# Two more adaLN blocks in the gated mixer, none in the last stages, and a pool residual without ScalarE's bias step

## The chip, the cores and the metric

The kernel runs on one core of one Trainium2 chip. The metric is the device time of one execution in microseconds (us). The median of three runs of the kernel before is 1438.69 us (1438.45 to 1440.27). All matrices are float32; the program is one straight line of instructions for each of the five engines (TensorE, VectorE, ScalarE, GpSimd, SyncE), tied together by semaphores that the author sets by hand.

## The reference

One inference step of a trunk of four layers, for 128 context tokens and 128 latent tokens with the same weights. D is 1024.

```
mod = silu(cond) @ w_ada[i] + b_ada[i]          # 1024 x 6144 per layer
sh1, sc1, g1, sh2, sc2, g2 = split(mod, 6)
h = rmsnorm(x) * norm_g * (1 + sc1) + sh1
x = x + g1 * mixer_i(h)        # 0: Hyena, 1: gated linear attention, 2: FNet, 3: pooling
h = rmsnorm(x) * norm_g * (1 + sc2) + sh2
x = x + g2 * hier_moe(h)       # 16 SwiGLU experts, hidden 512, two per token
pool mixer: y = ((window_mean(h) - h) @ pool_w + pool_b) * pool_scale
```

Each weight is read once from HBM; the profile counts 549 MB read.

## The kernel before

**Weights as pieces.** `piece_stream` (L118) writes down one order in which all weights come: pieces of 1 MB (128 partitions x 2048 floats) that SyncE loads into a ring of 14 slots. A slot is loaded again when TensorE has used what lay in it, and SyncE waits for the slots strictly in that order. From the second pair of experts on a layer loads expert pieces two at a time, as one transfer of 2 MB. Four further slabs of each layer (the second matrices of its first pair of experts) go to a place outside the ring; in layers 0 to 2 SyncE waits for a point in the mixer before it loads them.

**adaLN blocks.** w_ada is cut into 12 blocks of 2048 columns, three for each layer, and each block into 8 pieces. Block 3i gives sh1 and sc1 of layer i, block 3i+1 gives g1 and sh2, block 3i+2 gives sc2 and g2. `ada(n, lo, hi)` (L619) issues the matmuls of pieces lo to hi of block n on TensorE: four matmuls a piece (eight instructions in the profile), which write four strips of 32 partitions of one PSUM bank (line L626). When a block is complete, VectorE copies the bank to `rows` (`ada_rows`, L1370), TensorE turns it by four transposes (`ada_turned`, L630, line L634), and VectorE adds the bias and forms the scale (`ada_mod`, L1376). A new block may begin when the modulation of the block before it is formed, since it uses the same bank.

**Where they stand.** The blocks are put by hand between other work of TensorE. Block 5 and 6 lie in the projections of the gated mixer (`pe_gla`, L480): block 6 between the k and the v projections, its turn behind v, ahead of the gates of the backward direction. Block 7 lies at the mixer's end. Block 8 lies beside the norm behind the mixer and beside the routing of layer 1's experts (`residual` with beside=8, `moe(1, 8)`), with its turn behind the first gather. Layer 2 (FNet) has block 9 in the mixer and block 10 beside norm and routing. Layer 3 (pooling) has block 11 inside its mixer. Its routing has no block beside it.

**A layer's norm.** ScalarE squares x into hT, one of 8 column blocks at a time (`square`, L1087, line L1093). TensorE sums the squares over partitions with a matrix of ones (`norm`, `sum_squares`, line L640). ScalarE takes a logarithm and an exponential of the sum (`inverse_root`, L1099, lines L1101 and L1102). VectorE multiplies (L1394), then ScalarE shifts and scales the context tokens (L1115) and VectorE the latent ones (L1398). For the odd norms, those behind a mixer, GpSimd adds the squares of blocks 1 to 6 into block 0, so that TensorE sums two blocks only.

**A residual behind a mixer.** For each of the 8 column blocks m, ScalarE reads the mixer's output from PSUM, adds a bias and writes `yb` (`residual`, L1118, line L1124), VectorE adds the gated value to xT (L1401, line L1405), and ScalarE squares the new block. In the pool mixer VectorE's factor is the gate times pool_scale, and pool_b is ScalarE's bias.

**The experts.** `moe(i)` computes the routing: logits (L840), transposes of h (L845), a chain of small operations on VectorE (L1509 to L1547), and ranks (L865 to L869). The first gather (L685) selects token rows into 64 slots an expert. Then come eight pairs of experts in order (`moe_round`, L753). A pair is the first matrix (L720, 32 instructions), the scatter of the pair before (L703), the third matrix (L720), a gather for a later pair (L685), transposes (L727, L732), and the second matrix (L744, 32 instructions). At the end VectorE adds the sums from PSUM to xT (`sums_added`, line L1460).

Of the kernel before, what the change touches and what calls it, by code (L numbers as in the profile page):

```python
# [18 lines left out]
L = 128  # L19
# [18 lines left out]
COUPLES = PAIRS // 2  # L38
HALF = D // 8 + 1


# [76 lines left out]
def piece_stream():  # L118

    def ada(n, lo=0, hi=KD):  # L120
        return [("ada", n, k) for k in range(lo, hi)]

    def pieces(name, count):
        return [(name, c) for c in range(count)]

    before = [ada(0) + pieces("w_in", 12) + ada(1) + ada(2) + ada(3) + pieces("w_out", 4) + ada(4),
              ada(5, 0, 5) + pieces("wq", 2) + ada(5, 5) + pieces("wk", 2) + ada(6) + pieces("wv", 4)
              + pieces("wg", 4) + ada(7) + pieces("wo", 4) + ada(8),
              ada(9) + pieces("fn", 4) + ada(10),
              ada(11, 0, 5) + pieces("pool", 1) + ada(11, 5)]  # L130
    out, at = [], 0
    for i in range(LAYERS):
        experts = [("moe", i, p, kind, q) for p in range(PAIRS) for kind in range(3) for q in range(SLABS)
                   if p or kind < 2]
        for what in before[i] + [("first", i)] + experts + [("further", i)]:
            if what[0] in ("first", "further"):
                out.append((what, None, None))
                at += at % 2
                continue
            out.append((what, at % RING, at // RING))  # L140
            at += 1
    return out
# [11 lines left out]
def build(nc, a):  # L154
# [21 lines left out]
    with ctx:  # L176
# [35 lines left out]
        def vcol(name, lo, n=1):  # L212
            return vec[:, VEC[name] + lo:VEC[name] + lo + n]
# [266 lines left out]
        def pe_gla(pe, arrived, ada, ada_turned, norm, h_ready, project, residual):  # L480
# [25 lines left out]
            ada(6, 0, 8)  # L506
            for c in range(4):
                w8 = arrived(("wv", c), KD)
                for g in range(G):
# [6 lines left out]
                    if c % 2:  # L516
                        last.then_inc(s("gla_proj"), 1)
            ada_turned(6)
            gates(pe, 1)
            pe.wait_ge(s("v_ready"), 4)  # L520

            def g_tiles(first, end):

                pe.wait_ge(s("mod_ready"), 7)
                for m in range(first, end):
# [58 lines left out]
            pe.wait_ge(s("g_raw"), 8)  # L584
            ada(7, 0, 3)

            pe.wait_ge(s("upd_read"), 6)
            for h in range(HEADS):
# [4 lines left out]
                if h % 2:  # L593
                    last.then_inc(s("osum_mm"), 1)
            ada(7, 3, 8)
            residual(1, "wo", oT, lambda k: pe.wait_ge(s("o_ready"), k + 1), turned=7, beside=8)

# [11 lines left out]
        def _(pe):  # L609
# [35 lines left out]
            def norm(n, beside=None):  # L645

                if n % 2:
                    pe.wait_ge(s("squares_added"), (KD - 2) * (n // 2 + 1))
                for k in (0, KD - 1) if n % 2 else range(KD):
                    sum_squares(n, k)  # L650
# [343 lines left out]


            pe_gla(pe, arrived, ada, ada_turned, norm, h_ready, project, residual)
            moe(1, 8)


            ada(9, 0, 2)  # L1000
            norm(4)
            ada(9, 2, 5)
            pe.wait_ge(s("cm_loaded"), 16 * 2)
            cg = cm[:, 0:4 * HALF].rearrange("p (k n) -> p k n", k=2)
            cl, *sl = [cm[:, 4 * HALF + n * P:4 * HALF + n * P + P] for n in range(3)]
            for g in range(G):
                for r in range(4):
# [8 lines left out]
                    last.then_inc(s("mix_mm"), 1)  # L1016
            ada(9, 5, 8)
            pe.wait_ge(s("mix_rows"), 8)
            for m in range(KD):
# [5 lines left out]
                if m % 2:  # L1025
                    last.then_inc(s("mix_mm"), 1)
            ada_turned(9)
            pe.wait_ge(s("mix_rows"), 8 + 4)
            residual(2, "fn", rhs=fnm, beside=10)
            moe(2, 10)  # L1030


            ada(11, 0, 2)
            norm(6)
            ada(11, 2, 5)
            pw = arrived(("pool", 0), KD)
            pe.wait_ge(s("cm_loaded"), 16 * 3)
            for g in range(G):
                for r in range(4):
# [6 lines left out]
                    if r % 2:  # L1046
                        last.then_inc(s("mix_mm"), 1)
            ada(11, 5, 8)
            pe.wait_ge(s("mix_rows"), 12 + 4)
            for m in range(KD):  # L1050
# [3 lines left out]
                last.then_inc(s("res_mm"), 1)  # L1054
                if m == 1:
                    ada_turned(11)
            norm(7)
# [11 lines left out]
        def _(act):  # L1069
# [48 lines left out]
            def residual(i, bias, src):  # L1118
                for m in range(KD):
                    act.wait_ge(s("res_mm"), KD * i + m + 1 if i < 3 else KD * i + (m | 1) + 1)  # L1120
                    if m >= 4:
# [218 lines left out]
            for b in range(4):  # L1340
                act.wait_ge(s("mix_mm"), 12 + b + 1)
                act_fn(plr[:, b // 2, 2 * (b % 2):2 * (b % 2) + 2], bank[b][:].rearrange("p (r n) -> p r n", r=2),
                       ACT.Copy).then_inc(s("mix_rows"), 1)
            residual(3, "pool_b", half)
            moe(3)
# [10 lines left out]
        def _(dve):  # L1356
# [392 lines left out]
            v.memset(sc[:], 0.0).then_inc(s("sc_clear"), 1)  # L1749
            ada_rows(6)  # L1750
            ada_mod(6)
            scores(0)
# [15 lines left out]
            for m in range(KD):  # L1768
                dve.wait_ge(s("ors_ready"), m // 4 + 1)
                o = oT[:, m].rearrange("p g t -> p (g t)")  # L1770
                tt(o, o, ors[:, m // 2], ALU.mult).then_inc(s("o_ready"), 1)
            ada_rows(7)
            residual(1, g1(1))
            ada_mod(7)
            moe(1, 8)
            norm(4)
            ada_rows(9)
            residual(2, g1(2))
            ada_mod(9)
            moe(2, 10)  # L1780
            norm(6)
            ada_rows(11)
            ada_mod(11)

            gs = rtv(200, KD, G)
            chain(tt(gs, mod[:, 3, 16:24], vcol("pool_scale", 0, KD).unsqueeze(2).broadcast_to([P, KD, G]), ALU.mult))
            residual(3, lambda m, g: gs[:, m, g:g + 1])
            moe(3)
# [10 lines left out]
        def _(pool):  # L1799
# [17 lines left out]
            add_squares(5)  # L1817
            add_squares(7)

# [84 lines left out]
```

## Time and profile before

| | |
|---|---|
| median of 3 runs | 1438.69 us |
| the profiled execution: time, span | 1437.99 us, 1436.2 us |
| TensorE matmul busy | 1357.9 us (95%) |
| VectorE, ScalarE, GpSimd busy | 361.1, 286.8, 36.4 us |
| DMA | 552.28 MB, 385 GB/s in the mean |
| chain that ended last | PE 80%, DMA 15%, DVE 2%, ACT 1% |

The span runs from the first to the last instruction of the profile; the time of the same execution is 1.8 us longer. Names of engines in the rows are PE (TensorE's matmuls), PEld (its weight loads), DVE (VectorE), ACT (ScalarE), POOL (GpSimd) and SP (SyncE). L626 is line 626 of the kernel. A row of a timeline may merge several instructions of one kind, and its length is then that of all of them together. A matmul's length holds the time in the pipeline, so that matmuls overlap; what one costs is best read from the start of the next. The PEclk column is the granted clock of TensorE, 1.00 being 2.4 GHz and 0.50 being 1.2 GHz.

### The profile page before, as it was taken

The page shows a single profiled execution, that of the slowest core. Times are in us where ns is not written, and L with a number is a line of the kernel's source. Part 1 is how long each engine was busy: PE and PEld are TensorE (multiplying, and loading weights), DVE is VectorE, ACT ScalarE, POOL GpSimd, SP SyncE. Part 2 cuts the span into 40 slices and gives each one's busy share as a digit, 9 for nine tenths or more (in the row PEclk, how much of TensorE's full clock was granted, in tenths as well). Part 3 has the DMA queues.
Part 4 walks back from the last instruction along what each step waited for, and adds up shares of the span by engine and source line. Part 5 has one row for each costly group of instructions (what it writes and reads, how often), then busy time and mean ns, then how long its engine had stood idle before and what let it go on. Part 6 is the DMA issues. An engine that isn't in the chain of part 4 may idle for free.

```text
span 1436.2 us, 17316 instructions
## 1 busy us (share of the span) xinstructions
PE 1357.9 (95%) x7234; PEld 734.6 (51%) x7234; DVE 361.1 (25%) x883; ACT 286.8 (20%) x523; POOL 36.4 (3%) x36
## 2 busy tenths in 40 slices
PE   7999999999989999999999989999998887999986
PEld 3786584444325788774444336744443353444433
DVE  3444514112113313323111113331111144111113
ACT  3211024111102221232111004421110054111101
POOL 0001310000000000010000000100000000000000
PEclk9999999999999999999999999999999997999998
DMA  9956999999999983499999999999999999999994
GB/s 377 420 194 226 404 398 384 395 424 429 427 427 421 421 371 103 186 410 385 396 427 427 428 426 420 421 428 421 426 428 428 426 419 401 383 427 428 427 428 167
DMA packets 54213, 552.28 MB, mean 385 GB/s; under 512 B 5937, under 2 KB 7921, under 8 KB 8817
## 3 DMA queue, kind: packets, MB, share of 16 engines
q1 hardware_dynamic: 52496, 549.09, 91.8%
q10 hardware_dynamic: 1634, 2.02, 0.4%
q8 instruction: 60, 0.98, 0.3%
q14 instruction: 23, 0.19, 0.0%
HBM read 548.99 MB, written 2.10 MB: 384 GB/s over the span
## 4 chain that ended last, share of the span: by engine, by line
PE 80%; DMA 15%; DVE 2%; ACT 1%; issue 0%; POOL 0%; SPq 0%; POOLq 0%; DVEq 0%
PE bank L720 25%; PE bank L666 14%; DMA ring<-in_moe_w 12%; PE bank L744 12%; PE bank L626 5%; PE bank L685 4%; PE bank L703 3%; DMA ring<-in_pool_w 2%; PE bank L497 2%; PE bank L514 2%; PE bank L640 1%; PE bank L840 1%; PE bank L952 1%; PE bank L572 1%; PE bank L727 1%; PE bank L890 1%
## 5 line engine op out<-in xcount | busy, mean ns | idle before, releaser
L720 PE MATMUL bank<-ring,arena 128*64 128x512 f32 x1024 | 229.4, 595 | 33.0 <-DMA ring<-in_moe_w 31.4
L720 PE MATMUL bank<-ring,hT 128*64 128x512 f32 x1024 | 225.3, 594 | 0.0
L744 PE MATMUL bank<-ring,arena 128*64 128x512 f32 x896 | 198.8, 596 | 0.0
L720 PEld LDWEIGHTS bank<-ring,arena 128*64 128x64 f32 x1024 | 73.1, 137 | 181.6 <-issue 151.4
L720 PEld LDWEIGHTS bank<-ring,hT 128*64 128x64 f32 x1024 | 72.1, 137 | 139.3 <-issue 137.0
L1430 DVE TENSOR_TENSOR rows<-rows,bank 128x512 f32<-128x512 f32 x32 | 22.0, 688 | 469.4 <-PE bank L720 469.4
L744 PEld LDWEIGHTS bank<-ring,arena 128*64 128x64 f32 x896 | 61.2, 137 | 117.6 <-issue 112.0
L666 PE MATMUL bank<-hT,ring 128*128 128x256 f32 x512 | 112.4, 380 | 0.0
L666 PEld LDWEIGHTS bank<-hT,ring 128*128 128x128 f32 x512 | 96.5, 190 | 15.2 <-issue 2.5
L1152 ACT ACTIVATE yv_big<-bank,arena 128x512 fp32r<-128x512 f32 x64 | 44.0, 688 | 288.6 <-PE bank L744 288.6
L1449 DVE SCALAR_TENSOR_TENSOR yv_rest<-bank,arena,yv_big 128x512 fp32r<-128x512 f32 x64 | 48.1, 751 | 200.1 <-ACT yv_big L1152 200.1
L626 PE MATMUL bank<-ring,condT 128*32 128x512 f32 x768 | 91.1, 602 | 6.5 <-DMA ring<-in_w_ada 4.8
L666 PE MATMUL bank<-arena,ring 128*128 128x256 f32 x384 | 83.8, 380 | 1.2 <-DVE arena L1642 0.9
L666 PEld LDWEIGHTS bank<-arena,ring 128*128 128x128 f32 x384 | 72.6, 190 | 12.2 <-DVE arena L1642 1.2
L685 PE MATMUL bank<-sel,htok_big 128*128 128x256 f32 x256 | 69.4, 305 | 1.7 <-DVE sel L1417 1.7
L703 PE MATMUL bank<-selT,yv_big 128*128 128x256 f32 x256 | 66.6, 297 | 1.7 <-DVE yv_rest L1449 1.7
L685 PE MATMUL bank<-sel,htok_rest 128*128 128x256 f32 x256 | 64.6, 286 | 0.0
L703 PEld LDWEIGHTS bank<-selT,yv_big 128*128 128x128 f32 x256 | 48.0, 187 | 28.5 <-issue 26.0
L703 PE MATMUL bank<-selT,yv_rest 128*128 128x256 f32 x256 | 62.1, 279 | 0.0
L685 PEld LDWEIGHTS bank<-sel,htok_big 128*128 128x128 f32 x256 | 49.4, 193 | 23.9 <-issue 20.7
L1145 ACT ACTIVATE rows<-bank 128x512 f32<-128x512 f32 x32 | 19.1, 597 | 211.4 <-PE bank L720 211.4
L1135 ACT ACTIVATE arena<-bank 128x512 f32<-128x512 f32 x32 | 19.1, 598 | 157.9 <-PE bank L685 157.9
(215 smaller groups left out, 1225.7 us busy)
## 6 DMA issues: line engine op xcount, KB each, us to landing
ring<-in_moe_w SPq DMA_DIRECT2D x166, 2048.0 KB, 19.4
ring<-in_w_ada SPq DMA_DIRECT2D x96, 1024.0 KB, 22.5
ring<-in_moe_w SPq DMA_DIRECT2D x36, 1024.0 KB, 20.3
arena<-in_moe_w SPq DMA_DIRECT2D x16, 1024.0 KB, 19.6
ring<-in_hy_w_in SPq DMA_DIRECT2D x12, 1024.0 KB, 28.0
ring<-in_hy_w_out SPq DMA_DIRECT2D x4, 1024.0 KB, 12.0
ring<-in_gla_w_v SPq DMA_DIRECT2D x4, 1024.0 KB, 22.7
ring<-in_gla_w_g SPq DMA_DIRECT2D x4, 1024.0 KB, 16.5
```

The source lines that it names most:

```text
L497: last = mm(half(4 * w + h), w8[:, k, (h % 2) * P:(h % 2) * P + P], hT[:, k].rearrange("p g t -> p (g t)"), start=k == 0, stop=k == KD - 1)
L514: last = mm(bank[b][:, 256 * (c % 2):256 * (c % 2) + 256], hT[:, k, g], w8[:, k, :], start=k == 0, stop=k == KD - 1)
L626: last = mm(ada_bank(n)[32 * j:32 * j + 32, :], condT[:, G * k:G * k + 32], w[:, j, :], start=k == 0, stop=k == KD - 1)
L666: last = mm(dst, w[:, k, (m % 2) * P:(m % 2) * P + P], (hT[:, k] if rhs is None else rhs[:, k]).rearrange("p g t -> p (g t)"), start=k == ...
L685: last = mm(bank[b][:, (k % 2) * NT:(k % 2) * NT + NT], htok[n % 2][:, n // 2, k * P:k * P + P], sel[:, n // 2].rearrange("p e j n -> p (e ...
L703: last = mm(half(m), part[:, m * P:m * P + P], selT[:], start=first_pair and m % 2 == 0 and part is yv[0], stop=False, skip_group_check=True)
L720: last = mm(bank[4 + kind][SLOTS * e:SLOTS * e + SLOTS, :], x[:, k, at:at + SLOTS], w[:, kk, e, :], start=k == 0, stop=k == KD - 1)
L744: last = mm(bank[6 + q // 2][SLOTS * e:SLOTS * e + SLOTS, :], hidT[:, f, SLOTS * e:SLOTS * e + SLOTS], w[:, ff, e, :], start=f == 0, stop= ...
L1135: act_fn(dst[:, 2 * t:2 * t + 2], bank[b][:].rearrange("p (k n) -> p k n", k=2), ACT.Copy) \
L1152: act_fn(yv[0][:, 512 * h:512 * h + 512], bank[6 + h][:], ACT.Identity, scale=wcol) \
L1430: tt(sil[:], sil[:], bank[5][:], ALU.mult).then_inc(s(pre + "hid_ready"), 1)
L1449: stt(yv[1][:, cols], bank[6 + h][:], wcol, yv[0][:, cols].bitcast(F32), ALU.mult, ALU.subtract) \
```

## The change

The order of the pieces and TensorE's program change so that blocks 7 and 8 come inside the gated mixer's v projection and behind it, and each later block moves up. Block 6 is turned behind the first quarter of v. Block 7 is issued behind the second quarter and turned behind the third. Block 8 is issued behind v and turned behind the gates of the backward direction. Block 9 takes block 7's place at the mixer's end, block 10 takes block 8's place beside norm and routing of layer 1. In layer 2 block 11 stands in block 9's place and nothing beside norm and routing. Layer 3 has no block.

In the pool mixer ScalarE no longer copies and biases. VectorE forms gain times bias, adds it to all of xT in one instruction while the pooling is still to come, and then updates each block straight from PSUM. ScalarE squares only. For this norm (7) TensorE sums all eight blocks and GpSimd none.

```diff
@@ piece_stream
-              ada(5, 0, 5) + pieces("wq", 2) + ada(5, 5) + pieces("wk", 2) + ada(6) + pieces("wv", 4)
-              + pieces("wg", 4) + ada(7) + pieces("wo", 4) + ada(8),
-              ada(9) + pieces("fn", 4) + ada(10),
-              ada(11, 0, 5) + pieces("pool", 1) + ada(11, 5)]
+              ada(5, 0, 5) + pieces("wq", 2) + ada(5, 5) + pieces("wk", 2) + ada(6) + pieces("wv", 2) + ada(7)
+              + pieces("wv", 4)[2:] + ada(8) + pieces("wg", 4) + ada(9) + pieces("wo", 4) + ada(10),
+              ada(11) + pieces("fn", 4),
+              pieces("pool", 1)]
@@ TensorE, gated mixer
             for c in range(4):
+                if c == 1:
+                    ada_turned(6)
+                if c == 2:
+                    ada(7, 0, 8)
+                if c == 3:
+                    ada_turned(7)
                 w8 = arrived(("wv", c), KD)
...
-            ada_turned(6)
+            ada(8, 0, 8)
             gates(pe, 1)
+            ada_turned(8)
             pe.wait_ge(s("v_ready"), 4)
             def g_tiles(first, end):
-                pe.wait_ge(s("mod_ready"), 7)
+                pe.wait_ge(s("mod_ready"), 9)
...
-            ada(7, 0, 3)
+            ada(9, 0, 3)
...
-            ada(7, 3, 8)
-            residual(1, "wo", oT, lambda k: pe.wait_ge(s("o_ready"), k + 1), turned=7, beside=8)
+            ada(9, 3, 8)
+            residual(1, "wo", oT, lambda k: pe.wait_ge(s("o_ready"), k + 1), turned=9, beside=10)
@@ TensorE, norm: POOLED = (1, 3, 5)
-                if n % 2:
+                if n in POOLED:
                     pe.wait_ge(s("squares_added"), (KD - 2) * (n // 2 + 1))
-                for k in (0, KD - 1) if n % 2 else range(KD):
+                for k in (0, KD - 1) if n in POOLED else range(KD):
@@ TensorE, layers 1 to 3 (each ada(9, ...) of layer 2 is an ada(11, ...) now)
-            moe(1, 8)
+            moe(1, 10)
...
-            residual(2, "fn", rhs=fnm, beside=10)
-            moe(2, 10)
-            ada(11, 0, 2)
+            residual(2, "fn", rhs=fnm)
+            moe(2)
             norm(6)
-            ada(11, 2, 5)
...
-            ada(11, 5, 8)
             pe.wait_ge(s("mix_rows"), 12 + 4)
...
-                if m == 1:
-                    ada_turned(11)
@@ ScalarE, pool mixer
-            residual(3, "pool_b", half)
+            load_log_exp()
+            act_fn(minus[:], ident, ACT.Copy, scale=-1.0)
+            for m in range(KD):
+                square(7, m)
@@ VectorE, gated mixer
-            ada_rows(6)
-            ada_mod(6)
+            for n in (6, 7, 8):
+                ada_rows(n)
+                ada_mod(n)
             scores(0)
@@ VectorE, pool mixer
-            ada_rows(11)
-            ada_mod(11)
-            gs = rtv(200, KD, G)
-            chain(tt(gs, mod[:, 3, 16:24], vcol("pool_scale", 0, KD).unsqueeze(2).broadcast_to([P, KD, G]), ALU.mult))
-            residual(3, lambda m, g: gs[:, m, g:g + 1])
+            gs, gb = rtv(200, KD, G), rtv(216, KD, G)
+            wide = lambda name: vcol(name, 0, KD).unsqueeze(2).broadcast_to([P, KD, G])
+            chain(tt(gs, mod[:, 3, 16:24], wide("pool_scale"), ALU.mult))
+            chain(tt(gb, gs, wide("pool_b"), ALU.mult))
+            chain(tt(xT[:], xT[:], gb.unsqueeze(3).broadcast_to([P, KD, G, L]), ALU.add))
+            for m in range(KD):
+                dve.wait_ge(s("res_mm"), KD * 3 + (m | 1) + 1)
+                for g in range(G):
+                    last = stt(xT[:, m, g], half(m)[:, g * L:g * L + L], gs[:, m, g:g + 1], xT[:, m, g],
+                               ALU.mult, ALU.add)
+                last.then_inc(s("x_added"), 1)
@@ GpSimd
-            add_squares(7)
```

## Rows read from the trace of the kernel before

**Rows 1.** The chain of waits: start us, length us, and what.
```profile
656.01 13.88 PE bank L720 x64
672.64 7.02 PE bank L744 x32
...
698.38 7.02 PE bank L744 x32
...
857.09 7.07 PE bank L744 x32
...
943.20 13.88 PE bank L720 x64
...
1211.00 13.88 PE bank L720 x64
...
1410.78 7.04 PE bank L744 x32
```

**Rows 2.** Windows: us, busy time of PE, PEld, DVE, ACT, POOL, clock, DMA share, GB/s.
```profile
441.00:530.00 89.00, 88.56 (x478) 63.65 (x475) 23.14 (x50) 23.30 (x40) 0.00 (x0) 1.00 1.01 420
530.00:600.00 70.00, 68.37 (x418) 58.63 (x417) 25.37 (x42) 19.79 (x30) 0.00 (x0) 1.00 0.32 112
1207.00:1210.00 3.00, 3.00 (x16) 3.00 (x15) 1.37 (x5) 0.87 (x2) 0.00 (x0) 0.50 0.98 415
```

**Rows 3.** Timeline of PE, gated mixer: start us, us, engine, line, operation, tiles.
```profile
492.79 7.07 PE L626 MATMUL bank<-ring,condT 128*32 128x512 f32 x64
499.79 27.89 PE L514 MATMUL bank<-ring,hT 128*128 128x256 f32 x128
527.52 0.60 PE L634 MATMUL bank<-base,rows 128*128 128x128 f32 x4
527.96 1.89 PE L605 MATMUL bank<-cm 128*128 128x256 f32 x8
```

**Rows 4.** Timeline of DVE, gated mixer; in brackets the idle time before.
```profile
499.93 0.69 DVE L1374 COPY rows<-bank 128x512 f32<-128x512 f32 x1 [0.82 <-PE bank L626]
...
528.16 0.19 DVE L1382 TENSOR_TENSOR mod<-bank,vec 128x32 f32<-128x32 f32 x1 [27.54 <-PE bank L634]
```

**Rows 5.** Timeline of PE's weight loads, end of layer 0's experts.
```profile
441.46 0.20 PEld L744 LDWEIGHTS bank<-ring,arena 128*64 128x64 f32 x4 [0.73 <-DMA ring<-in_moe_w]
```

**Rows 6.** Timeline of DVE and ACT, layer 2, second norm.
```profile
921.92 0.61 DVE L1405 SCALAR_TENSOR_TENSOR xT<-arena,mod,xT 128x128 f32<-128x128 f32 x2 [2.84 <-ACT arena L1124]
...
924.42 0.47 ACT L1101 ACTIVATE rstd<-bank,small 128x256 f32<-128x256 f32 x1 [1.44 <-PE bank L640]
```

**Rows 7.** Timeline of PE, layer 2, the first gather.
```profile
938.70 0.36 PE L685 MATMUL bank<-sel,htok_big 128*128 128x256 f32 x1 [0.19 <-DVE sel L1417]
```

**Rows 8.** Timeline of ACT, stage of layer 3.
```profile
1162.36 0.48 ACT L1101 ACTIVATE rstd<-bank,small 128x256 f32<-128x256 f32 x1 [2.22 <-PE bank L640]
...
1163.78 4.38 ACT L1115 ACTIVATE hT<-hT,mod,scale 128x128 f32<-128x128 f32 x8 [0.49 <-DVE hT L1394]
...
1191.57 0.47 ACT L1101 ACTIVATE rstd<-bank,small 128x256 f32<-128x256 f32 x1 [1.31 <-PE bank L640]
```

**Rows 9.** Timeline of PE and DVE, end of layer 2 and stage of layer 3.
```profile
1146.86 7.17 PE L744 MATMUL bank<-ring,arena 128*64 128x512 f32 x32
...
1155.46 4.22 DVE L1460 SCALAR_TENSOR_TENSOR xT<-bank,mod,xT 128x128 f32<-128x128 f32 x16
...
1165.27 7.31 PE L1045 MATMUL bank<-ring,hT 128*128 128x256 f32 x32 [0.24 <-DMA ring<-in_pool_w]
...
1175.23 1.16 PE L1052 MATMUL bank<-cm,arena 128*128 128x128 f32 x8
...
1205.45 0.36 PE L685 MATMUL bank<-sel,htok_big 128*128 128x256 f32 x1 [1.18 <-DVE sel L1417]
```

**Rows 10.** Timeline of DVE and ACT, last norm.
```profile
1419.23 4.22 DVE L1460 SCALAR_TENSOR_TENSOR xT<-bank,mod,xT 128x128 f32<-128x128 f32 x16
...
1424.69 0.47 ACT L1101 ACTIVATE rstd<-bank,small 128x256 f32<-128x256 f32 x1 [0.79 <-PE bank L640]
```

More of the change, by code:

```diff
@@ L39 @@
 HALF = D // 8 + 1
+POOLED = (1, 3, 5)
 VEC = {}
@@ L996, in _ @@
             pe_gla(pe, arrived, ada, ada_turned, norm, h_ready, project, residual)
-            moe(1, 8)
-            ada(9, 0, 2)
+            moe(1, 10)
+            ada(11, 0, 2)
             norm(4)
-            ada(9, 2, 5)
+            ada(11, 2, 5)
             pe.wait_ge(s("cm_loaded"), 16 * 2)
@@ L1016, in _ @@
                     last.then_inc(s("mix_mm"), 1)
-            ada(9, 5, 8)
+            ada(11, 5, 8)
             pe.wait_ge(s("mix_rows"), 8)
@@ L1026, in _ @@
                     last.then_inc(s("mix_mm"), 1)
-            ada_turned(9)
+            ada_turned(11)
             pe.wait_ge(s("mix_rows"), 8 + 4)
-            residual(2, "fn", rhs=fnm, beside=10)
-            moe(2, 10)
-            ada(11, 0, 2)
+            residual(2, "fn", rhs=fnm)
+            moe(2)
             norm(6)
-            ada(11, 2, 5)
             pw = arrived(("pool", 0), KD)
@@ L1119, in residual @@
                 for m in range(KD):
-                    act.wait_ge(s("res_mm"), KD * i + m + 1 if i < 3 else KD * i + (m | 1) + 1)
+                    act.wait_ge(s("res_mm"), KD * i + m + 1)
                     if m >= 4:
@@ L1771, in _ @@
                 tt(o, o, ors[:, m // 2], ALU.mult).then_inc(s("o_ready"), 1)
-            ada_rows(7)
+            ada_rows(9)
             residual(1, g1(1))
-            ada_mod(7)
-            moe(1, 8)
+            ada_mod(9)
+            moe(1, 10)
             norm(4)
-            ada_rows(9)
+            ada_rows(11)
             residual(2, g1(2))
-            ada_mod(9)
-            moe(2, 10)
+            ada_mod(11)
+            moe(2)
             norm(6)
-            ada_rows(11)
-            ada_mod(11)
-            gs = rtv(200, KD, G)
-            chain(tt(gs, mod[:, 3, 16:24], vcol("pool_scale", 0, KD).unsqueeze(2).broadcast_to([P, KD, G]), ALU.mult))
-            residual(3, lambda m, g: gs[:, m, g:g + 1])
+            gs, gb = rtv(200, KD, G), rtv(216, KD, G)
[9 more added lines that the diff above has]
+                last.then_inc(s("x_added"), 1)
             moe(3)
```

## Prediction

> **What bounds the kernel now.** I read the chain of waits first, in order of time. In each channel mixer (MoE) it walks over TensorE's expert matmuls, and only behind the last pairs over transfers of expert weights. One pair of experts costs TensorE 25.74 us, the step between two rows of L744 (672.64 to 698.38) [rows 1]. A round that never waits would come from its first expert matmul to the L744 of its eighth pair in 16.63 (656.01 to 672.64) + 7 x 25.74 = 196.8 us. Measured are 201.1 in layer 1 (656.01 to 857.09), 199.8 in layer 3 (1211.00 to 1410.78) [rows 1] and 203.7 in layer 2 (943.20 to 1146.86) [rows 1, 9]. So transfers lag by 4.3, 3.0 and 6.9 us at the end of these rounds, and all else of them is TensorE's own time.
>
> Next come the windows. DMA works at 420 GB/s from 441 to 530 us, but moves 112 GB/s from 530 to 600 in the gated mixer [rows 2]: 70 x (1 - 112/420) = 51.3 us of transfer time lie idle there, because the ring of 14 slots is full. TensorE is busy 68.37 of those 70 us [rows 2]. So the gated mixer is bound by TensorE, the MoE rounds nearly so, and the stretches between them by TensorE and short chains over ScalarE and VectorE (the timelines of rows 6 to 10 show them). A block that goes into the gated mixer is paid there in full, and earns what it gives back elsewhere. I sum along TensorE's program and give the transfers their part as the lag of each round.
>
> **1. Gated mixer, two more blocks.** Blocks 7 and 8 are new there; 9 and 10 take the places of 7 and 8. One block with its data at hand is 7.00 us (492.79 to 499.79), four transposes are 0.44 (527.52 to 527.96) [rows 3]. Two blocks are 14.0 and two more turns 0.9. The last turn stands right ahead of g_tiles, which wait for its modulation: VectorE starts that 0.64 us behind the transposes' start and needs 0.19 [rows 4], with the signal some 0.9, of which 0.44 is the transposes: +0.5. The other turns wait for nothing: VectorE has copied block 6 by 500.6 [rows 4], and its turn comes at 499.79 + 6.97 = 506.8 (a v group is a quarter of 27.89 [rows 3]); block 7's copy falls under the third v group. In VectorE's queue the new copies and modulations stand ahead of scores(0), in a time in which it idles. SP gets 16 more pieces to issue, into a ring that is full later anyway. Together **+15.4 us**, between +14.0 (the turns hidden) and +16.
>
> Does the data come? The last piece of layer 0's experts lands at 441.46 [rows 5]; at 420 GB/s a piece of 1.049 MB takes 2.50 us. The last piece of block 8 is the 40th: 441.46 + 99.9 = 541.4. TensorE wants it at 499.79 + 4 x 6.97 + 2 x 0.44 + 7.0 + 7/8 x 7.0 = 541.7. I take no wait, with 0.3 us to spare; this is the tightest place. 16 pieces are 39.9 us of transfer, so 51.3 - 39.9 + 15.4 = 26.8 us of idle transfers remain. The ring is again full behind it, and layer 1's round starts in its present state: lag 4.3 as now.
>
> **2. Stage of layer 2.** Block 11 takes block 9's place: nothing. Block 10 goes from the norm and the routing. In the norm, one piece of it delayed the last sum: VectorE's last update ends at 922.53 and the logarithm starts at 924.42, 1.89 later [rows 6]; where no block stands between it is 1.24 (1423.45 to 1424.69) [rows 10]. That gives -0.65. From the logarithm to the gather it takes 14.28 with a block (924.42 to 938.70) [rows 6, 7] and 13.88 without (1191.57 to 1205.45) [rows 8, 9]: -0.4. The turn behind the gather goes, -0.44 [rows 3]. Against these -1.5 stands the clock. In layer 3, where no block fills the routing, TensorE's granted clock is 0.50 (its level of 1.2 GHz) from 1207 to 1210 [rows 2], and the gather takes 5.5 us (1205.45 to 1211.00) instead of 938.70 to 943.20 less the turn, 4.0 [rows 1, 7, 9]: 1.5 us. Here it may cost 0 to 1.5, since that depends on where the idle time falls; I take 1.1, nearer to the one row that shows it. Sum: **-0.4**, between -1.5 and 0.
>
> The Trainium skill, "TensorE: Matmul & The Clock Gate", section "HAM oscillation — how this bites in real kernels", says that idle gaps between bursts of matmuls bring the clock down, so that the next burst starts slow. It speaks against taking the block out of the routing; the trace of layer 3 agrees, with 0.50 granted at the gather. By the rule alone the step is 0, without it -1.5.
>
> **3. Lag of layer 2's round.** Layer 1's last piece has been used by 857.09 + 7.07 = 864.2 [rows 1]. With 12 pieces in place of 20 ahead of the experts, 12 + 14 in the ring and the four slabs outside it are there 30 x 2.50 us later, by 939.2, and the round starts at 943.2 - 1.5 = 941.7: the ring is full before it. SP now meets its wait for the DFT, ahead of those slabs, eight pieces earlier; what that holds back would find no slot before the round anyway. The round then behaves as those of layers 1 and 3, with 4.3 and 3.0 in place of 6.9. I take 3.9: **-3.0**, between -2.6 and -3.9; no lag at all would be -6.9.
>
> **4. Stage of layer 3.** I follow it by its logarithms. The first one comes 2.68 behind VectorE's last sum (1159.68 to 1162.36) [rows 8, 9], because pieces of block 11 stand ahead; it will be 1.24, as at the end [rows 10]: 1160.9, -1.4. ScalarE's shifts then end at 1168.16 - 1.4 = 1166.7 [rows 8]. Behind the last shift stand 18 of the 32 matmuls of L1045, which take 7.31 together [rows 9]: 4.1, so 1170.8. A copy of 128x512 is 0.69 on VectorE [rows 4]; with some 0.9 for ScalarE's copy and its signals the pooling matmuls start at 1171.7 instead of 1175.23 [rows 9]. The pool weights are the first piece behind the experts, so the wait for them at 1165.27 [rows 9] is gone and the shifts are late next.
>
> The residual was a ring of ScalarE's bias step, VectorE's update and the square, and its logarithm stands at 1191.57 [rows 8]. Now VectorE reads PSUM itself, in the form of L1460: 16 in 4.22 us [rows 9, 10]. It can begin when the first pair of columns is pooled, 1.2 behind 1171.7 (1.16 for eight matmuls [rows 9]), and ends at 1177.1; TensorE makes each further pair in less than VectorE's 1.06. The logarithm follows 1.24 later, at 1178.3, with TensorE adding all eight squares as there; GpSimd's six additions are not waited for any more. So -13.3. The wide addition of gain times bias is one instruction over 2048 columns; at L1460's rate it takes 4.2 us at most and ends by 1171.4, under the copy of the pool rows. ScalarE's table load and negated identity lie under the pooling matmuls. If either cover failed, what sticks out is some 1 to 2 us. The gather stays at 5.5 or gets its clock back, 0 to -1.5, and I take -0.4, since the same routing stands before it. Sum: **-13.7**, between -11.5 and -15.
>
> **5. Layer 3's round.** It starts with a ring that is nearly full now and full then: 0, within 1.
>
> The sum is +15.4 - 0.4 - 3.0 - 13.7 = **-1.7 us** against the profiled execution (span 1436.2, time 1438.0): a span of 1434.5. The median of 1438.7 lies 0.7 above that execution; from it the same sum gives 1437.0 us. The ends of the terms, added, reach from -7.4 to +2.9.
>
> **The rivals.** *A, faster: the transfers give back more.* If it is the transfers that really set the rounds, the lag of all three goes (14.2 us, not 3.0) and the clock holds in both gathers (2.2 more): 1437.0 - 11.2 - 2.2 = 1423.6. The milder form, no lag in layer 2 (3.9 more) and both clocks, is 1430.9. For it: half of 51.3 us of idle transfers is filled. Against it: layer 1's round starts behind this idle time, with a full ring, and lags by 4.3.
>
> The Trainium skill, "Perfetto Trace Analysis", section "Optimization Strategy", says that a kernel whose most contended engine changes over time may gain by interleaving those regimes. By that alone the 24.5 us of idle transfers that are filled would be won, and the time be 1414. The trace disagrees: TensorE is busy through the stage with the idle transfers.
>
> *B, slower: the block behind v runs dry.* The pieces come in order. If one takes over 2.51 us, TensorE waits in block 8, and everything behind it with it. Each per cent is 1.0 us: at 2.62 (400 GB/s) the last piece is 4.6 us late, the sum is +2.9, and with both gathers slow +3.7: 1442.4. For it: 0.3 us to spare. Against it: 420 GB/s over the 89 us around it.
>
> *C, slower: the residual doesn't shrink.* ScalarE's squares now follow each update directly, as its bias steps did. If the two still take turns and keep 1.1 us per block in place of 0.53, it adds 4.6: 1441.6. Against it: the same pair of steps at the end of a round goes at 0.53 per block (4.22 for eight) with the logarithm 1.24 behind [rows 10].
>
> **Numbers.** This kernel's time can be told from no change beyond 0.2%, 2.9 us. Forecast 0.66, its own range 1434 to 1439.5; A 0.22, mostly in its milder form; B 0.08; C 0.04. Of the forecast some 0.1 falls below 1435.8. So faster 0.32, same 0.57, slower 0.11. The range, 1431.5 to 1441, holds most of A's milder form and leaves out the far ends.
>
> **What would show it.** Layer 1's first expert matmul at 656.0 + 15.4 = 671.4, its lag still 4.3; 27 us of idle transfers in the gated mixer; layer 2's round near 200.7 us; a clock of 0.50 near its gather; the pooled updates in some 4.2 us, and no wait for pool weights. I am wrong if TensorE waits for w_ada near 541, if the pooled residual takes over 5 us, or if a full ring leaves a lag far from 3 to 4.3.

## The result, and the profile after

Measured are 1441.61 us (median of 12, 1440.48 to 1443.43) against 1438.24 before (12 runs beside them, 1436.82 to 1440.27): ratio 1.0024, 95% interval 1.0015 to 1.0032. The change costs 3.4 us (95%: 2.2 to 4.6), where I forecast a gain of 1.7. The profiled execution after took 1442.39 us, 0.8 above its median.

The page after: the granted clock (in tenths) and DMA's rate in 40 slices of 36 us. In the gated mixer only one slice, the 17th, is left with 128 GB/s, and the clock dips in two slices, the 27th (layer 2's routing and gather) and the 34th, that of layer 3:
```profile
span 1440.2 us, 17318 instructions
...
PEclk9999999999999999999999999989999998999999
...
GB/s 381 420 182 221 404 400 386 388 426 428 428 427 421 421 420 420 128 390 383 384 428 426 427 427 422 353 302 381 428 427 426 428 421 309 382 429 427 426 428 186
```

The chain of waits, the rows that answer to [rows 1] (L728 was L720, L752 was L744):
```profile
235.39 13.88 PE bank L728 x64
...
673.71 13.88 PE bank L728 x64
...
874.77 7.11 PE bank L752 x32
...
961.95 13.88 PE bank L728 x64
...
1163.19 7.11 PE bank L752 x32
...
1216.44 13.88 PE bank L728 x64
...
1415.57 7.04 PE bank L752 x32
```
The kernel before has, at the head of the same chain:
```profile
234.12 13.88 PE bank L720 x64
```
Read as differences between one row and the next (before: this row and those of [rows 1, 9]), they split the time into the steps of the prediction:

| stretch | before | after | change | forecast |
|---|---|---|---|---|
| start to round of layer 0 | 234.12 | 235.39 | +1.3 | 0 |
| layer 0's round to layer 1's (gated mixer) | 421.89 | 438.32 | +16.4 | +15.4 |
| round of layer 1 | 201.08 | 201.06 | 0.0 | 0 |
| stage of layer 2 | 86.11 | 87.18 | +1.1 | -0.4 |
| round of layer 2 | 203.66 | 201.24 | -2.4 | -3.0 |
| stage of layer 3 | 64.14 | 53.25 | -10.9 | -13.7 |
| round of layer 3 | 199.78 | 199.13 | -0.7 | 0 |
| behind it | 25.42 | 24.63 | -0.8 | 0 |
| span | 1436.2 | 1440.2 | +4.0 | -1.7 |

The first and the last row hold no changed instruction, and between executions they vary by about this much (layer 0's round starts between 233.93 and 236.28 in the runs below). The second row holds layer 0's round too, which no edit touches and which took 203.90 us before and 204.15 after; from its last L744 (L752) on, the gated mixer's part is +16.2.

In windows (the columns as in [rows 2]), the gated mixer does what it should, and the two stages behind it do not. From 530 to 620 the transfers now move 291 GB/s, before 181. In the routing of layer 2 (936 to 950), in its gather (956 to 960) and all through the gather of layer 3 (1210 to 1214) the granted clock is low:
```profile
530.00:620.00 90.00, 87.83 (x544) 70.27 (x546) 26.61 (x46) 22.31 (x33) 0.00 (x0) 1.00 0.73 291
936.00:950.00 14.00, 10.54 (x45) 6.06 (x43) 6.33 (x22) 6.55 (x15) 0.72 (x1) 0.76 1.02 428
...
958.00:960.00 2.00, 2.00 (x12) 2.00 (x11) 1.33 (x5) 0.60 (x1) 0.00 (x0) 0.55 0.00 0
...
1210.00:1212.00 2.00, 2.00 (x11) 2.00 (x11) 1.66 (x11) 0.23 (x1) 0.00 (x0) 0.50 0.75 320
```

TensorE's timeline shows the end of v in the gated mixer: block 8, the one wait for its last piece, and a short one between the last turn and g_tiles:
```profile
537.20 6.22 PE L634 MATMUL bank<-ring,condT 128*32 128x512 f32 x56
543.89 1.06 PE L634 MATMUL bank<-ring,condT 128*32 128x512 f32 x8 [0.47 <-DMA ring<-in_w_ada]
544.88 1.99 PE L613 MATMUL bank<-cm 128*128 128x256 f32 x8
546.72 0.60 PE L642 MATMUL bank<-base,rows 128*128 128x128 f32 x4
547.64 2.61 PE L674 MATMUL bank<-hT,ring 128*128 128x256 f32 x11 [0.33 <-issue]
```

### The profile page after: what moved, and what is told of

Same layout as the page of the kernel before. It is cut to its first block, busy times and chain, and to the rows that moved or that the text cites. A ratio compares the mean times of both kernels' runs of the same rounds, so it can differ in the third digit from the quotient of the medians.

```text
span 1440.2 us, 17318 instructions
## 1 busy us (share of the span) xinstructions
PE 1366.1 (95%) x7246; PEld 740.0 (51%) x7246; DVE 361.8 (25%) x885; ACT 283.3 (20%) x515; POOL 32.1 (2%) x30
## 4 chain that ended last, share of the span: by engine, by line
PE 79%; DMA 17%; DVE 2%; ACT 1%; issue 0%; POOL 0%; SPq 0%; DVEq 0%; POOLq 0%
PE bank L728 24%; DMA ring<-in_moe_w 14%; PE bank L674 14%; PE bank L752 12%; PE bank L693 4%; PE bank L634 4%; PE bank L711 3%; PE bank L498 2%; PE bank L648 2%; DMA ring<-in_w_ada 2%; PE bank L848 1%; PE bank L960 1%; PE bank L521 1%; PE bank L584 1%; PE bank L580 1%; PE bank L735 1%
## 5 line engine op out<-in xcount | busy, mean ns | idle before, releaser
L728 PE MATMUL bank<-ring,arena 128*64 128x512 f32 x1024 | 228.9, 595 | 30.3 <-DMA ring<-in_moe_w 29.0
L728 PE MATMUL bank<-ring,hT 128*64 128x512 f32 x1024 | 225.4, 594 | 0.0
L752 PE MATMUL bank<-ring,arena 128*64 128x512 f32 x896 | 198.9, 596 | 0.2 <-DMA ring<-in_moe_w 0.2
L728 PEld LDWEIGHTS bank<-ring,arena 128*64 128x64 f32 x1024 | 73.0, 137 | 178.3 <-issue 150.3
L728 PEld LDWEIGHTS bank<-ring,hT 128*64 128x64 f32 x1024 | 72.0, 137 | 139.5 <-issue 136.5
L752 PEld LDWEIGHTS bank<-ring,arena 128*64 128x64 f32 x896 | 61.1, 137 | 118.0 <-issue 112.0
L693 PEld LDWEIGHTS bank<-sel,htok_rest 128*128 128x128 f32 x256 | 51.7, 202 | 0.0
## 6 DMA issues: line engine op xcount, KB each, us to landing
ring<-in_hy_w_in SPq DMA_DIRECT2D x12, 1024.0 KB, 26.8
ring<-in_gla_w_g SPq DMA_DIRECT2D x4, 1024.0 KB, 26.8
```

The costliest lines, as they stand in the source:

```text
L693: last = mm(bank[b][:, (k % 2) * NT:(k % 2) * NT + NT], htok[n % 2][:, n // 2, k * P:k * P + P], sel[:, n // 2].rearrange("p e j n -> p (e ...
L728: last = mm(bank[4 + kind][SLOTS * e:SLOTS * e + SLOTS, :], x[:, k, at:at + SLOTS], w[:, kk, e, :], start=k == 0, stop=k == KD - 1)
L752: last = mm(bank[6 + q // 2][SLOTS * e:SLOTS * e + SLOTS, :], hidT[:, f, SLOTS * e:SLOTS * e + SLOTS], w[:, ff, e, :], start=f == 0, stop= ...
```

## The experiments

Eight kernels ran, each beside the kernel before on the same chip. The theory is that the rounds and the mixer are TensorE's, so that an added block costs its 7 us, and that what I got wrong is the clock. The rival is that transfers, or the timing of the ring, set the time.

**The pool residual alone.** The kernel before, with the new residual; the blocks stay where they were, the wide addition stands ahead of block 11's copy and modulation.
```diff
-            residual(3, "pool_b", half)
+            load_log_exp()
+            act_fn(minus[:], ident, ACT.Copy, scale=-1.0)
+            for m in range(KD):
+                square(7, m)
...
+                for g in range(G):
+                    last = stt(xT[:, m, g], half(m)[:, g * L:g * L + L], gs[:, m, g:g + 1], xT[:, m, g],
+                               ALU.mult, ALU.add)
```


> The pool residual alone, on the kernel before; all adaLN blocks stay where they were (block 11 in the pool mixer, its modulation formed ahead of the updates). Theory 1 (the residual delivers, and the moved blocks cost more than they give back): in the kernel after, the logarithm of norm 7 comes 7.3 us behind the start of the pooling matmuls (1188.07 to 1195.40), in the one before 16.3 (1175.23 to 1191.57). With block 11's turn in between I expect some 7.8, so 8.5 us less: 1429.7 us, at most 1431. Theory 2 (the residual is no gain by itself, it only looks so because no block stands in layer 3): 1436 or more. Transfers as the bound (theory 3): layer 3's round would lag more and give part back, 1433 or more.


Measured: 1433.36 us against 1438.45, ratio 0.9962 (0.9948 to 0.9976): -5.1. Its chain:
```profile
1202.04 13.88 PE bank L721 x64
...
1405.61 7.04 PE bank L745 x32
```
Layer 3's round starts 9.0 us earlier than in [rows 1], as the first theory had it (8.5), but its last L745 starts only 5.2 earlier, and the time of 1433.4 is a miss for that theory (1429.7, at most 1431) and lies where the third put it: the round takes 203.6 us in place of 199.8. The groups of that round say what took most of these 3.8 us back. In the kernel before, and then in this one (busy time and mean of one, then the idle time before them by what ended it):
```profile
L720 PE MATMUL bank<-ring,arena 128*64 128x512 f32 x256 | 57.2, 595 | 6.1 <-DMA ring<-in_moe_w 6.1
```
```profile
L721 PE MATMUL bank<-ring,arena 128*64 128x512 f32 x256 | 57.5, 596 | 9.5 <-DMA ring<-in_moe_w 8.7 <-issue 0.8
```
The round meets a ring that has had 9 us less to fill, with block 11 still in the queue ahead of it: up to its start the transfers run without a pause (425 GB/s from 1180 to 1202), while in the changed kernel they all but stop ahead of it (41 GB/s from 1212 to 1214), the ring being full. So the residual is worth 9 us on TensorE's side, and 5 as long as the transfers lag.

**The blocks alone.** The changed kernel with the old residual (the edit above, reversed).


> The moved blocks alone: the kernel after with the pool residual of before. Theory 1: 9.0 us above the kernel after, 1450.6 us; layer 1's first expert matmul some 16 us later than before, of which layer 2 and 3 give back only about 4. Theory 2: as the kernel after, 1441 to 1443. Theory 3 (transfers set the rounds): the later start is caught up, 1440 to 1445.


Measured: 1448.78 us, ratio 1.0069 (1.0055 to 1.0083): +10.3, forecast at +12. The parts, -5.1 and +10.3, add up to +5.2, and the whole costs 3.4: with the blocks moved, layer 3's round takes 199.1 us behind the early start too (203.6 with the residual alone), so nothing of the residual is given back. In layer 3's stage the residual is worth 62.16 - 53.25 = 8.9 us there. The times show less of it, 1448.78 - 1441.61 = 7.2 (these medians were not taken side by side; against the kernel before beside each it is 10.3 - 3.4 = 6.9): 1.0 of the rest is layer 2's stage, the same instructions in both, which took 86.17 us here and 87.18 in the changed kernel.

**The clock in layer 2's stage.** The changed kernel with 28 matmuls on data long at hand, into a bank that nobody reads: twelve behind the norm's sums, sixteen in the routing. They leave the output as it is.
```diff
+            def fill(pieces):
+                for _ in range(pieces):
+                    for j in range(4):
+                        mm(bank[7][32 * j:32 * j + 32, :], condT[:, 0:32], cm[:, 0:512], start=True, stop=True)
...
+                if n in [5]:
+                    pe.wait_ge(s("mod_ready"), 12)
+                    fill(3)
...
+                if i in [2]:
+                    fill(2)
```


> The kernel after with 28 extra matmuls of an adaLN block's form on resident data (seven pieces' worth, no transfer) beside layer 2's second norm and routing, where block 10 stood before. Their result is not used. Theory 1 (TensorE idles there, its granted clock falls to 0.50, the logits take 1.0 us and the gather 1.6 us longer): clock 1.00 in both, gather 3.9 us instead of 5.5, at a cost of some 0.4 us where a filler delays the ranks; 2.1 us less than the kernel after, 1439.5. If the clock is not what cost the time in layer 2: the fillers come on top or hide, 1441.6 to 1442.5.


Measured: 1439.47 us, ratio 1.0002 (0.9992 to 1.0011), as expected. Layer 2's stage takes 85.03 us, in place of 87.18.

**The clock in both stages.** The same, and again in layer 3 (`n in [5, 7]`, `i in [2, 3]`; in the trace each of the 28 is two).


> The same fillers in layer 2 and in layer 3. Theory 1: layer 3's gather falls from 6.75 to 3.9 us and its logits by 0.4, with 0.4 lost beside the ranks: 2.8 us below the run with fillers in layer 2 only, 1436.7. If the clock is not the cause: no less than the kernel after, 1441.6 to 1443.


Measured: 1437.52 us, ratio 0.9992 (0.9983 to 1.0002); expected were 1436.7. The second set is worth 1439.47 - 1437.52 = 1.95 us, where 2.8 were expected. The windows of the routing and gather of both layers, and TensorE in layer 2's:
```profile
936.00:950.00 14.00, 12.77 (x83) 6.56 (x85) 6.82 (x28) 7.91 (x17) 0.73 (x1) 1.00 1.02 429
950.00:965.00 15.00, 14.81 (x103) 7.34 (x97) 7.05 (x34) 6.61 (x13) 0.00 (x0) 1.00 0.50 189
...
1195.00:1210.00 15.00, 14.81 (x110) 7.87 (x102) 10.99 (x53) 9.03 (x20) 0.00 (x0) 1.00 0.93 395
```
```profile
940.57 2.78 PE L648 MATMUL bank<-cm,condT 128*32 128x512 f32 x24
943.17 4.10 PE L856 MATMUL bank<-hT,rw 128*32 128x256 f32 x16
...
955.13 0.28 PE L701 MATMUL bank<-sel,htok_rest 128*128 128x256 f32 x1
955.25 0.28 PE L701 MATMUL bank<-sel,htok_big 128*128 128x256 f32 x1
```
In the changed kernel the same sixteen matmuls of the logits and the same steps of the gather are:
```profile
943.66 4.84 PE L848 MATMUL bank<-hT,rw 128*32 128x256 f32 x16 [2.23 <-DVE hT L1404]
...
1210.46 0.41 PE L693 MATMUL bank<-sel,htok_rest 128*128 128x256 f32 x1
1210.68 0.41 PE L693 MATMUL bank<-sel,htok_big 128*128 128x256 f32 x1
```
A gather matmul starts every 0.12 us at full clock, every 0.21 at 0.50. With the clock held, the stages take 85.05 us (layer 2) and 50.44 (layer 3): my steps gave 86.11 - 0.4 = 85.7 and 64.14 - 13.7 = 50.4. Holding the clock takes 1441.61 - 1437.52 = 4.1 us away, of which my steps had 1.1 - 0.4 = 0.7 in them already.

**The routing alone.** The kernel with 28 matmuls in layer 2, without the twelve matmuls behind the norm (`fill(0)`).


> The kernel after with the fillers of layer 2's routing only (four pieces' worth), none beside its norm. Theory 1, by place: the clock is full in the gather (5.5 to 3.9 us) and still 0.50 in the logits behind the norm (1.0 us): 1440.4, between the kernel after and the run with all fillers of layer 2 (1439.5). If a single stretch of idle time is behind both: 1439.5 or 1441.6.


Measured: 1440.13 us, ratio 1.0006 (0.9997 to 1.0016). Layer 2's stage takes 85.00 us here and 85.03 there, although this one's clock still falls to 0.88 from 936 to 950:
```profile
936.00:950.00 14.00, 10.50 (x58) 5.82 (x60) 7.09 (x29) 7.92 (x18) 0.72 (x1) 0.88 1.02 430
950.00:965.00 15.00, 14.81 (x99) 7.40 (x93) 6.78 (x33) 6.30 (x12) 0.00 (x0) 1.00 0.48 181
```
The expectation was that the logits would then still cost 1.0 us, and the stage does not show it. Without the twelve the logits take 4.35 us in place of 4.10, but start 2.23 us behind the logarithm in place of 2.49, and the gather comes 14.27 us behind it in place of 14.28. The times can't tell the two kernels apart. This does not settle whether the twelve would help where the clock falls further, as in the changed kernel, whose logits took 4.84.

This kernel also shows that the low clock does not keep its place. Layer 3's stage is the changed kernel's here, instruction for instruction, and takes 52.74 us in place of 53.25, with the gather at 5.55 us in place of 6.76, but with a slower pool projection, under which the clock was 0.50 from 1178.1 to 1180.1. The projection in the changed kernel, and in this one:
```profile
1179.32 8.06 PE L1051 MATMUL bank<-ring,hT 128*128 128x256 f32 x32 [2.20 <-DVE hT L1404]
```
```profile
1176.12 9.15 PE L1065 MATMUL bank<-ring,hT 128*128 128x256 f32 x32 [2.20 <-DVE hT L1418]
```
All kernels in which a stage has the changed kernel's instructions, one profiled execution of each, and the stages with the added matmuls beside them ("way" is from the logarithm of the norm behind the mixer to the gather, "proj." the pool projection; us):

| kernel | layer 2's stage | way, gather | layer 3's stage | proj., way, gather |
|---|---|---|---|---|
| changed | 87.18 | 14.91, 5.56 | 53.25 | 8.06, 14.28, 6.76 |
| blocks alone | 86.17 | 13.94, 5.54 | (old residual) | |
| block 7 doubled (below) | 87.02 | 13.96, 6.43 | 52.50 | 8.89, 13.89, 5.55 |
| 28 matmuls in layer 2 | 85.03, clock held | 14.28, 4.06 | 53.24 | 8.06, 14.28, 6.76 |
| routing alone | 85.00, clock held in part | 14.27, 4.05 | 52.74 | 9.15, 13.87, 5.55 |
| 28 in both | 85.05, clock held | 14.26, 4.06 | 50.44, clock held | 8.06, 14.19, 4.06 |

So the same instructions lose to the clock in one place or another, 1.1 to 2.2 us against the held clock in layer 2's stage and 2.1 to 2.8 in layer 3's. What decides the place no run shows.

**Seven us of TensorE without a byte.** The changed kernel issues each matmul of block 7 twice, the second time into a bank that is overwritten later. TensorE's work grows as if by a block, transfers don't.
```diff
+                    if n == 7:
+                        again(n, k)
...
+            def again(n, k):
+                w = ring[where["ada", n, k][0]].rearrange("p (k n) -> p k n", k=4)
+                for j in range(4):
+                    mm(bank[6][32 * j:32 * j + 32, :], condT[:, G * k:G * k + 32], w[:, j, :], start=True, stop=True)
```


> The kernel after with every matmul of block 7 (in the middle of v) issued twice, the extra ones into an unused PSUM bank: TensorE's work of a third extra block, and not a byte more of transfers. Theory 1 (a block in the gated mixer costs what TensorE needs for it, to the end of the kernel): 7.0 us more, less the 0.5 us that TensorE waits for block 8's last piece now: 1448.1 us. Theory 3 (the transfers set where the rounds end, a block costs because of its bytes): 1441.6 to 1443.


Measured: 1446.94 us against 1439.38, ratio 1.0052 (1.0037 to 1.0068), where 1448.1 was expected. That is 7.6 above the kernel before, of which the changed kernel has 3.4, so 4.2 are the doubling's; the medians of the two, not taken side by side, differ by 5.3. Block 7 with its double takes 13.87 us, and block 8 waits for nothing:
```profile
514.69 1.07 PE L643 MATMUL bank<-ring,condT 128*32 128x512 f32 x8
...
528.56 7.17 PE L521 MATMUL bank<-ring,hT 128*128 128x256 f32 x32
...
543.01 7.07 PE L636 MATMUL bank<-ring,condT 128*32 128x512 f32 x64
```
From layer 0's round to layer 1's there are 5.6 us more than in the changed kernel (443.93 and 438.32), of 6.9 put in. Of the rest 0.47 is the wait that went, and 0.6 lies ahead of the doubled block, in layer 0's round, which both kernels share (203.55 us here, 204.15 in the changed kernel); behind that round the mixer takes 6.2 us more (240.38 and 234.17), so 0.2 is open. It is TensorE's time that the mixer costs, not the transfers'.

**Residual and clock together, blocks in place.** The pool residual alone, with the 28 matmuls in layer 3's stage.


> The pool residual alone on the kernel before, and fillers beside norm 7 and layer 3's routing. In the run with the residual alone layer 3's round starts 9.0 us earlier than before and ends 5.2 earlier, its lag grew from 3.0 to 6.8. Theory of the lag (that round now ends with the transfers): the fillers bring its first expert matmul forward by 1.4 us or so, and the end stays, 1433.0 to 1433.6 us. Theory 1 without the lag (TensorE's place decides): 1431.9.


Measured: 1434.21 us, ratio 0.9964 (0.995 to 0.9978), as without them (0.9962); the theory of the lag had 1433.0 to 1433.6, the other 1431.9. From logarithm to round layer 3's stage takes 18.26 us, without them 19.76 (clock 0.84 from 1180 to 1202, here 1.00), and the round 205.04 in place of 203.57. What the clock gives, the lag takes back:
```profile
1180.00:1202.00 22.00, 21.81 (x152) 12.38 (x152) 14.52 (x65) 13.61 (x30) 0.00 (x0) 1.00 1.02 422
```

**One block moved in place of two.** Block 7 in the middle of v, 8 at the mixer's end, 9 beside layer 1's norm and routing, 10 in the FNet mixer, 11 beside layer 2's norm and routing; none in layer 3's stage, with the new residual and the 28 matmuls there.
```diff
-            moe(1, 10)
+            moe(1, 9)
...
-            residual(2, "fn", rhs=fnm)
-            moe(2)
+            residual(2, "fn", rhs=fnm, beside=11)
+            moe(2, 11)
```


> The kernel after with one block moved, not two: block 7 in the middle of v, block 8 at the mixer's end, 9 beside layer 1's routing, 10 in layer 2's mixer, 11 beside layer 2's norm and routing, none in layer 3, and fillers beside norm 7 and layer 3's routing. From the terms measured: +7.9 in the gated mixer, nothing in layer 2 with its block and its lag of 6.9 as before, -13.5 in layer 3's stage with the clock held, -0.6 in its round, whose ring is full: -6.2 on the kernel before, 1432.2 us. If the ring's state doesn't matter (transfers never set the end), as much. If a block costs more in the gated mixer than one turn and 7.0 us: 1433 to 1435.


Measured: 1432.59 us, ratio 0.9959 (0.9945 to 0.9972), under both the kernel before and the changed one; 1432.2 was expected. Its chain, and its windows in the stages of layers 2 and 3:
```profile
234.95 13.88 PE bank L734 x64
...
663.88 13.88 PE bank L734 x64
...
866.24 7.08 PE bank L758 x32
...
1205.90 13.88 PE bank L734 x64
...
1405.73 7.04 PE bank L758 x32
```
```profile
926.00:940.00 14.00, 13.11 (x73) 6.33 (x72) 6.15 (x21) 6.51 (x14) 0.76 (x2) 1.00 1.01 419
940.00:955.00 15.00, 14.81 (x112) 9.04 (x113) 8.97 (x44) 8.48 (x16) 0.00 (x0) 1.00 1.02 428
1185.00:1210.00 25.00, 24.81 (x166) 12.91 (x166) 13.80 (x61) 14.26 (x29) 0.00 (x0) 1.00 0.72 304
```
Layer 3's round begins 5.1 us earlier than before and its last L758 starts 5.0 earlier, so nothing is given back. The first block added to the gated mixer moves layer 1's round by 428.93 - 421.89 = 7.0 us, the second by 438.32 - 428.93 = 9.4. But with one block layer 1's round itself takes 202.4 us (663.88 to 866.24), where all nine other kernels need 200.6 to 201.1. Up to the end of that round the first block costs 631.29 - 622.97 = 8.3 us and the second 639.38 - 631.29 = 8.1; one execution each doesn't show the second to be dearer. Against the kernel with the same residual and the same 28 matmuls but the blocks in place, the moved block costs these 8.3 us and gets back 4.4 between the starts of layer 2's and layer 3's rounds (257.97 and 253.56) and 5.2 in layer 3's round (205.04 and 199.83). Block 11 fills layer 2's routing and keeps the clock at 1.00 with useful work. This kernel, the residual alone and the residual with its clock held (0.9959, 0.9962, 0.9964) can't be told apart by their times.

## Why the prediction was wrong

**Gated mixer (+15.4; +16.4 measured).** The mechanism held: two blocks at 7.0, transfers that fill their idle time and give nothing for it. Idle transfers from 530 to 620 went from 90 x (1 - 181/420) = 51.2 us to 90 x (1 - 291/421) = 27.8 (forecast 26.8). The last turn cost 0.92 (546.72 to 547.64), as worked out. Beyond it are 0.47 us of waiting for the last piece of block 8, where I had given 0.3 to spare, and 0.3 in v, which took 28.03 us in four groups and 27.73 in one run ([rows 3], 499.79 to 527.52); the 0.25 left over is layer 0's round, not the mixer. One of my signs of being wrong, a wait for w_ada near 541, did come, at 543.4. Rival B names this wait; it came at a tenth of its price. Layer 1's first expert matmul stands at 673.7, forecast at 671.4, of which 1.3 is the later start. "Its lag still 4.3" holds: 201.06 against 196.8.

**Stage of layer 2 (-0.4; +1.1). This step failed.** The norm's -0.65 came (the logarithm, at 924.42 in [rows 6], stands at 941.48, 17.06 later, and the round ahead of it ended 17.68 later). The clock cost more than the 1.1 us that I had put in for it. I priced it at one place, the gather. It fell first under the logits (4.84 us in place of 4.10) and again under the gather (5.56 in place of the 4.0 of [rows 7]), and the way from the logarithm to the gather took 14.91 us, where 13.88 was forecast. The routing's -0.4 itself was right: in two other kernels with these instructions (blocks alone, block 7 doubled), in which the logits took 4.40, the way is 13.94 and 13.96. Over the three kernels the stage is 0.1, 0.9 and 1.1 us longer than before in place of 0.4 shorter, so against the -1.5 of the other terms the clock cost 1.6 to 2.6 us: my "1.1, nearer to the one row that shows it" was 0.5 to 1.5 too little, and my 0 to 1.5 was too narrow. Holding the clock with the 28 matmuls gives back less, 2.1 us (87.18 and 85.03), since they delay the gather themselves: 14.28, as with the block. The row of 13.88 came from a stage whose logits had paid already. In the kernel before, layer 2's logits and layer 3's are
```profile
926.91 4.10 PE L840 MATMUL bank<-hT,rw 128*32 128x256 f32 x16
...
1193.69 4.40 PE L840 MATMUL bank<-hT,rw 128*32 128x256 f32 x16 [2.16 <-DVE hT L1398]
```
I carried the price of that stage's gather over and did not ask what each burst ahead of it would pay.

**Lag of layer 2's round (-3.0; -2.4).** 203.66 became 201.24, a lag of 4.4, just above the 3.0 to 4.3 that a full ring was to leave.

**Stage of layer 3 (-13.7; -10.9). This step failed by its last term, the gather's -0.4, and by 0.8 ahead of it.** Its first half went as written: the logarithm 1.5 earlier, the pooling matmuls 10.91 behind it (forecast 10.8), the updates in 4.23 us (4.22). The rows of VectorE, TensorE and ScalarE that decide the rest:
```profile
1183.27 2.29 DVE L1794 TENSOR_TENSOR xT<-xT,arena 128x2048 f32<-128x2048 f32 x1
1189.34 4.23 DVE L1798 SCALAR_TENSOR_TENSOR xT<-bank,arena,xT 128x128 f32<-128x128 f32 x16 [3.78 <-PE bank L1057]
```
```profile
1188.07 3.84 PE L1057 MATMUL bank<-cm,arena 128*128 128x128 f32 x32 [0.69 <-ACT arena L1345]
1191.75 3.62 PE L648 MATMUL bank<-hT,ones 128*128 128x256 f32 x16
...
1197.52 4.80 PE L848 MATMUL bank<-hT,rw 128*32 128x256 f32 x16 [2.16 <-DVE hT L1404]
```
```profile
1189.98 4.03 ACT L1096 ACTIVATE hT<-xT 128x256 f32<-128x256 f32 x8 [0.34 <-DVE xT L1798]
1195.40 0.47 ACT L1104 ACTIVATE rstd<-bank,small 128x256 f32<-128x256 f32 x1 [1.39 <-PE bank L648]
```
VectorE ends at 1193.57, and the logarithm comes 1.83 later, not 1.24: TensorE's sixteen sums stand in its program behind all pooling matmuls and start only at 1191.75, 1.8 us behind the first square, and take 3.62 in a row. I had called GpSimd's additions "not waited for any more" and not asked when TensorE gets to the ones that took their place. That is 0.6, and small ones ahead of it are 0.2. Between logarithm and gather it takes 0.4 more than before (14.28 for the 13.88 of [rows 8, 9]), with the logits at 4.80 us. And the gather ran at 0.50 almost throughout: 6.76 us (1209.68 to 1216.44) in place of the 5.55 before, where I had taken 0.4 off: 1.6. With the 28 matmuls in both stages the same gather takes 4.06 (1206.97 to 1211.03). The residual's size was right, the clock's sign was wrong. How the clock's part splits is not firm: in two more kernels with these instructions (routing alone, block 7 doubled) the gather took 5.55 us and the way to it 13.9, but the pool projection 9.15 and 8.89 in place of 8.06, and the stage 52.74 and 52.50. So the stage missed by 2.1 to 2.8 us, 0.8 of it by the late sums and 1.3 to 2.0 by the clock.

**The rivals.** A is excluded: 51 us of idle transfers became 28, no round lost its lag, and block 7 doubled shows that 6.9 us of TensorE without a byte lengthen the mixer by 6.2 and the time by 4.2 to 5.3. C is excluded: 4.23 us for the updates. The mechanism with the larger part was in the text under step 2, as a term with too low a price, and beside step 4 with a gain in place of a loss; among the rivals only B's far end had both gathers slow, at 0.8 us together. Against the profiled execution the misses are +1.0 in the mixer, +1.5, +0.6 and +2.8 behind it, -0.7 in the last round, and +0.5 at the two ends: 5.7 us between -1.7 and +4.0. The kernel that takes the clock's loss away (28 matmuls in both stages) stands at 1437.5 where I had 1437.0; that they agree within 0.5 is partly luck, since what I had put in for the clock stands against what I had too little in the mixer and for the late sums.

The section of the Trainium skill that I cited against step 2, "HAM oscillation — how this bites in real kernels" ("TensorE: Matmul & The Clock Gate"), agrees with these rows, 0.50 granted behind the idle routing. I cited it and then let it cost 0 in layer 3's gather. The rule of interleaving in the Trainium skill, "Perfetto Trace Analysis", "Optimization Strategy", would have had 24.5 us for the filled transfers; the runs show none from that alone, since in the kernel before TensorE was busy 88.56 of the 89 us up to 530 [rows 2] and 88.37 of the 90 behind it, and each block needs 7.0 us of it.

What stays open: why the same instructions lose their clock under the logits, the pool projection or the gather from one kernel to the next; 0.2 of the doubled block's 6.9 us; why layer 1's round is 1.3 us longer with one block moved; and whether one block moved is better than the residual alone.

## What to carry to other kernels

Work moved out of a stretch of short chains took the clock with it here: price every burst of matmuls behind the gap that it leaves, at both levels of the clock (here 0.21 and 0.12 us per step), and not only the last. Which burst pays can change where nothing in the stage has changed. In this kernel idle transfers were worth filling only as far as later stages and rounds gave the block's time back: with the clock held, one block cost 8.3 us up to the end of layer 1's round and got 9.6 back behind it, which is within the noise of not moving it; the second cost 8.1 more and got less back (ratio 0.9992 in place of 0.9959). A stage that was shortened ahead of a round in which transfers lag gave back part of its gain (9.0 became 5.2), so a part tried alone and the part in its place are not worth the same.

## What the runs showed that I had not expected

- Nearly the whole gather of layer 3 was run at the lower level: 28 of its 32 steps at 0.21 us, although TensorE worked without a gap from the first of them. In the 15 us ahead of it (1195 to 1210) TensorE had been busy 9.51. In two other kernels the same gather took 5.55 us in place of 6.76, and the pool projection paid instead.
- 28 matmuls that compute nothing, in the trace 56 rows with 6.8 us of busy time (2.78 + 1.92 + 1.06 + 1.06 in layer 2), put where TensorE was idle, saved 2.1 us in one stage (87.18 against 85.03) and 2.1 to 2.8 in the other (52.50 to 53.25 against 50.44); by the medians 2.1 and 1.95.
- One execution and the next differ by up to 2.3 us before the first expert matmul (233.93 and 236.28), against an effect of 3.4. Differences between two rows of one execution are the safer reading.
